# Router logits from unnormed residual tiles, and the first output projection by token halves in its second column half

## The reference

```python
x = x + merged @ w_out[l]                       # first block
xn = rms_norm(x, ffn_norm_g[l])
gate, up = jnp.split(xn @ w_gate_up[l], 2, axis=-1)
x = x + (jax.nn.silu(gate) * up) @ w_down[l]
...
x = x + g1 * gated_merge(...)                   # second block
hx2 = modulate(rmsnorm(x, norm2_g[layer]), sh2, sc2)      # h * (1 + scale) + shift
...
logits = jnp.einsum('btd,de->bte', h, w_router)           # h is hx2, 16 experts
affinity = jax.nn.softmax(logits, axis=-1)
gate, idx = lax.top_k(jnp.swapaxes(affinity, 1, 2), cap)  # 128 tokens an expert
xe = jax.vmap(lambda hb, ib: hb[ib])(h, idx)
```

## Time and profile before

| | |
|---|---|
| median of 3 runs | 2959.38 us (2957.32 to 2959.53) |
| the profiled execution | 2959.49 us |
| its span | 2957.7 us, mean granted TensorE clock 0.978 |
| busy: TensorE, VectorE, ScalarE, GpSimd | 95%, 62%, 45%, 18% |
| TensorE | 13918 matmuls, 2816.5 us |

### The profile page before, as it was taken

One profiled execution on the slowest core, in us unless ns is written; L12 is line 12 of the kernel. 1 busy time (PEld: TensorE's weight loads), 2 busy tenths in 40 slices (PEclk: granted clock), 3 DMA queues, 4 the chain that ended last, 5 costly groups with the idle time before them and its releaser, 6 DMA issues.

```text
span 2957.7 us, 34913 instructions
## 1 busy us (share of the span) xinstructions
PE 2816.5 (95%) x13918; PEld 2239.1 (76%) x13918; DVE 1823.6 (62%) x2525; ACT 1332.3 (45%) x1934; POOL 522.4 (18%) x433
## 2 busy tenths in 40 slices
PE   7999998999999999999999999999999389999997
PEld 6777776788778778888887666667888278888885
DVE  5344534788775688642323555554445669999997
ACT  4344432333233455211112666664223257777775
POOL 0001202555554011330000111111000201000000
PEclk9999999999999999999999999999999689999998
DMA  4110131345652994321211111115324579999996
GB/s 153 40 44 29 43 107 71 100 135 157 185 164 96 354 262 140 114 57 50 67 62 40 44 40 43 33 43 170 111 98 152 220 264 392 391 398 398 395 397 236
DMA packets 256485, 465.76 MB, mean 157 GB/s; under 512 B 28812, under 2 KB 135444, under 8 KB 255812
## 3 DMA queue, kind: packets, MB, share of 16 engines
q1 hardware_dynamic: 229648, 377.00, 36.3%
q0 software_dynamic: 26528, 86.50, 9.2%
q10 hardware_dynamic: 148, 0.04, 0.0%
HBM read 409.91 MB, written 53.58 MB: 157 GB/s over the span
## 4 chain that ended last, share of the span: by engine, by line
PE 88%; DVE 6%; ACT 2%; DMA 2%; issue 2%; POOL 0%; SPq 0%; POOLq 0%; DVEq 0%; ACTq 0%
PE PS L129 82%; PE PS L132 5%; DVE m L138 3%; ACT m L135 1%; DVE m L144 1%; DMA m<-in_w_down_dram 1%; ACT L135 0%; DVE m L180 0%; DVE m L183 0%; DVE m L177 0%; SPq L186 0%; POOL m L138 0%; DMA m<-h_scratch 0%; DVE m L147 0%; DMA m<-in_x_dram 0%
## 5 line engine op out<-in xcount | busy, mean ns | idle before, releaser
L129 PE MATMUL PS<-m,m 128*128 128x512 f32 (+6 forms) x12102 | 2629.8, 390 | 39.5 <-DVE m L138 24.5
L129 PEld LDWEIGHTS PS<-m,m 128*128 128x128 f32 (+3 forms) x12102 | 2035.1, 184 | 558.9 <-issue 118.7
L135 ACT ACTIVATE m<-m 128x512 fp32r<-128x512 f32 (+5 forms) x722 | 735.6, 1041 | 818.6 <-PE PS L129 432.3
L138 DVE TENSOR_TENSOR m<-m,m 128x512 fp32r<-128x512 f32 (+7 forms) x714 | 909.6, 1304 | 268.4 <-ACT m L135 230.5
L135 ACT ACTIVATE m<-PS 128x512 f32<-128x512 f32 (+4 forms) x507 | 282.2, 579 | 515.0 <-PE PS L129 343.8
L138 DVE TENSOR_TENSOR m<-PS,m 128x512 fp32r<-128x512 f32 (+1 forms) x356 | 233.1, 684 | 334.1 <-PE PS L129 300.9
L138 POOL TENSOR_TENSOR m<-m,m 128x512 f32<-128x512 f32 (+3 forms) x164 | 260.1, 1589 | 579.9 <-DVE small L147 210.2
L132 PE MATMUL PS<-ident,m 128*128 128x128 f32 x1592 | 225.2, 281 | 80.6 <-DVE m L153 36.0
L132 PEld LDWEIGHTS PS<-ident,m 128*128 128x128 f32 x1592 | 193.5, 145 | 119.3 <-DVE m L153 36.3
L135 ACT ACTIVATE m<-m,small 128x640 f32<-128x640 f32 (+4 forms) x199 | 156.3, 788 | 220.9 <-DVE small L141 153.9
L147 DVE CUSTOM_DVE_ANT_0 m<-PS,m 128x640 f32<-128x640 f32 (+4 forms) x192 | 146.4, 775 | 119.3 <-PE PS L129 119.3
(11 more groups left out here) (83 smaller groups left out, 487.8 us busy)
## 6 DMA issues: line engine op xcount, KB each, us to landing
m<-in_w_exp_gate_dram SPq DMA_DIRECT2D x64, 1024.0 KB, 8.5
m<-in_w_exp_up_dram SPq DMA_DIRECT2D x64, 1024.0 KB, 8.6
m<-in_w_exp_down_dram SPq DMA_DIRECT2D x64, 1024.0 KB, 8.1
m<-in_w_mod_dram SPq DMA_DIRECT2D x48, 512.0 KB, 3.8
m<-in_w_gate_up_dram SPq DMA_DIRECT2D x44, 512.0 KB, 6.5
m<-in_w_in_dram SPq DMA_DIRECT2D x41, 512.0 KB, 4.1
m<-in_w_in_dram SPq DMA_DIRECT2D x12, 1024.0 KB, 5.2
h_scratch<-m POOLq DMA_DIRECT2D x22, 512.0 KB, 3.6
```

What stands on the lines that cost most here:

```text
L129: return Unsent() if self.e is None else self.e.matmul(o, l, r, start=first, stop=last, **k)
L135: return Unsent() if self.e is None else self.e.activation(o, i, fn, **k)
L138: return Unsent() if self.e is None else self.e.tensor_tensor(o, a, b, op)
```

## The change

**First output projection.** The second column half is done by token halves: tiles 0 to 3 with both halves of the contraction, then tiles 4 to 7. The means, roots and scales of tiles 0 to 3, the splits of the weights for `P1`, `P2`, `P6`, `P7`, and the transposes and splits of `B11` and `B21` move into this second half. `ffn_pe` begins with `P1` and `P2`. The orders of ScalarE, VectorE and GpSimd for block 0 follow: `T1` comes before `B22`, `P5` earlier, and GpSimd makes all of `T3` before `T2`.

**Router.** TensorE transposes the residual tile itself, before its norm (`x3T`), one half as soon as that column half is added. The gain A goes into the router's weights (`wr2`), and s @ W is one product for all tiles (`shift`, from a tile `sh2b` that repeats s in all columns, made by VectorE). The transposed tile is stationary now and the 16 columns of `wr2` pass through it, so that logits come with tokens in the partitions; VectorE multiplies them by r and adds the shift (`choose`), and the copy and the transpose back are gone. For tile 7 the normed tile is made after the softmax, by ScalarE and GpSimd. A and s come as columns through two small DMAs and two small transposes.

```diff
+        WO_ORDER = [(0, 0, 6), (0, 0, 7)] + [(0, 1, i) for i in range(NT)] + [
+            (1, kg, i) for i0 in (0, 4) for kg in range(2) for i in range(i0, i0 + 4)]
...
+            for c, kg, i in WO_ORDER:
+                pe.wait_ge(*(("zu_low", i) if kg else ("at_low", i)))
+                tok_group(pe, W_O + 2 * c + kg, i, 4 * kg, 4, 8, mlhs, "wo_acc", (c, kg, i), ("x1_half", c, i))
+                if (c, kg, i) == (1, 0, 7):
+                    pe.turn, pe.kept = 0, range(4, 8)
+                    turn_first(pe, 0)
+                elif (c, kg) == (1, 1) and 4 <= i < 7:
+                    turn_first(pe, i - 3)
+            pe.turn, pe.kept = 0, ()
...
-                if c:
-                    for P in "P1 P2 P6 P7".split():
-                        gu_high(act, 0, P)
...
+                    if c and i >= 4:
+                        xn_high(act, "B11", i - 4)
+                        xn_high(act, "B21", i - 4)
+                        if i == 4:
+                            gu_high(act, 0, "P6")
+                            gu_high(act, 0, "P7")
                     act.wait_ge("x1_half", c, i)
                     square(act, x1[:, i, half512(c)], ssq[:, i, c:c + 1], "x1", i, c)
-                    if (c, i) == (1, 6):
+                    if (c, i) == (1, 3):
                         root_of(act, ssum[:, 0:4], "x1", 0)
+                        gu_high(act, 0, "P1")
+                        gu_high(act, 0, "P2")
...
-                    if (c, i) == (1, 5):
+                    if (c, i) == (1, 3):
                         x1_mean(dve, 0)
+                        inverse_of(dve, ssum[:, 0:4], rs8[:, 0:4], "x1", 0)
+                        for i_ in range(4):
+                            xt1_scale(dve, i_)
+                        gu_low(dve, 0, "P1")
+                        gu_low(dve, 0, "P2")
...
         def ffn_pe(pe):
-            for i in range(4):
-                turn_xn(pe, "B11", i)
-                turn_xn(pe, "B21", i)
-            for i in range(4):
-                turn_xn(pe, "B22", i)
             gu_product(pe, 0, "P1")
-            for i in range(4):
-                turn_xn(pe, "T1", i)
             gu_product(pe, 0, "P2")
-            for i in range(4):
-                turn_xn(pe, "T3", i)
+            for T in "T1 B22 T3".split():
+                for i in range(4):
+                    turn_xn(pe, T, i)
+            gu_product(pe, 0, "P5")
+            pe.kept = (bank_of["gu_acc", 0, "P5"],)
             for i in range(4):
                 turn_xn(pe, "T2", i)
             gu_product(pe, 0, "P7")
-            gu_product(pe, 0, "P5")
+            pe.kept += (bank_of["gu_acc", 0, "P7"],)
             for i in range(4):
                 turn_xn(pe, "T4", i)
-            for P in "P6 P4 P3".split():
+            for P in "P6 P4".split():
                 gu_product(pe, 0, P)
+            gu_product(pe, 0, "P3")
+            pe.kept = ()
...
+            gu_high(act, 0, "P5")
             root_of(act, ssum[:, 4:8], "x1", 1)
-            for i in range(4):
-                xn_high(act, "B11", i)
-                xn_high(act, "B21", i)
-            for P in "P5 P4 P3".split():
+            for P in "P4 P3".split():
                 gu_high(act, 0, P)
-            for i in range(4):
-                xn_high(act, "B22", i)
             gu_first(act, 0)
-            for i in range(4):
-                xn_high(act, "T1", i)
             gu_silu0(act, 0)
-            for T in "T3 T2 T4".split():
+            for T in "T1 B22 T3 T2 T4".split():
                 for i in range(4):
                     xn_high(act, T, i)
...
         def ffn_dve(dve):
-            inverse_of(dve, ssum[:, 0:4], rs8[:, 0:4], "x1", 0)
-            xt1_scale(dve, 0)
-            xt1_scale(dve, 1)
             x1_mean(dve, 1)
-            xt1_scale(dve, 2)
-            xt1_scale(dve, 3)
+            gu_low(dve, 0, "P5")
             inverse_of(dve, ssum[:, 4:8], rs8[:, 4:8], "x1", 1)
             for i in range(4):
-                xn_low(dve, "B11", i)
-                xn_low(dve, "B21", i)
                 xt1_scale(dve, 4 + i)
                 xn_diff_dve(dve, i)
-            for P in "P5 P4 P3".split():
+            for P in "P4 P3".split():
                 gu_low(dve, 0, P)
-            for T in "B22 T1 T3 T2 T4".split():
+            for i in range(4):
+                xn_low(dve, "T1", i)
+            for T in "B22 T3 T2 T4".split():
                 for i in range(4):
                     xn_low(dve, T, i)
-            for c in range(22):
+            gu_u2(dve, 0)
+            gu_u3(dve, 0)
+            gu_c22(dve, 0)
+            gu_c21(dve, 0)
+            for P in "P1 P6".split():
+                gu_low(dve, 1, P)
+            gu_c12(dve, 0)
+            for P in "P2 P7 P5 P4 P3".split():
+                gu_low(dve, 1, P)
+            for c in range(1, 22):
...
         def ffn_pool(pool):
-            for i in range(4):
-                xn_diff_pool(pool, "T3", i)
-                xn_diff_pool(pool, "T2", i)
-            for i in range(4):
-                xn_diff_pool(pool, "T4", i)
+            for T in "T3 T2 T4".split():
+                for i in range(4):
+                    xn_diff_pool(pool, T, i)
...
+            pool.wait_ge("o2_out", 14)
+            for a, c in enumerate((4, 3)):
+                pool.dma_start(a2raw[0:8, a, :], rows_dram[0, 1024 * c:1024 * c + 1024].rearrange("(k p) -> k p", p=128)).then_inc(
+                    *pool.landed("grows_in"))
...
+                 ("out", 7, 1, 0, 4), ("route", 6, 0, 8), ("turn", 7, 0), ("choose", 6), ("out", 7, 1, 4, 8),
+                 ("pair", 2), ("route", 7, 0, 4), ("turn", 7, 4), ("norm", 7), ("route", 7, 4, 8), ("choose", 7), ("pair", 3)]
...
+            b = pe.bank("a2_cols")
+            bank_of["a2_turned",] = b
+            pe.wait_ge("grows_in")
+            for a in range(2):
+                t = pe.transpose(PS[:, b, 8 * a:8 * a + 8], a2raw[0:8, a, :], ident[0:8, 0:8])
+            t.then_inc(*pe.did("a2_turned"))
...
+                elif what == "shift":
+                    b = pe.bank("lc_out")
+                    bank_of["lc_acc",] = b
+                    pe.wait_ge("sh2_spread")
+                    pe.wait_ge("wr_in")
+                    for k in range(8):
+                        t = pe.matmul(PS[:, b, 0:16], sh2b[:, k, :], wr[:, k, :], k == 0, k == 7)
+                    t.then_inc(*pe.did("lc_acc"))
                 elif what == "turn":
-                    pe.wait_ge("hx2", i)
-                    for k0 in (0, 4):
-                        turn4(pe, xt3[i % 3], k0, 4, "hx2_turned", (i, k0), hx2_out(i, k0))
+                    k0 = part[0]
+                    pe.wait_ge("x3_half~", i, k0 // 4)
+                    turn4(pe, x3b[i % 4], k0, 4, "x3_turned", (i, k0), x3T_out(i, k0))
...
-                elif what == "choose":
-                    b = pe.bank("lg_shifted", i)
-                    bank_of["lg_turned", i] = b
-                    pe.wait_ge("lg_out", i)
-                    pe.transpose(PS[:, b, 0:16], lgT[0:16, :], ident[0:16, 0:16]).then_inc(*pe.did("lg_turned", i))
+                    k0, k1 = part
+                    if k0 == 0:
+                        bank_of["lg_acc", i] = pe.bank("lg_raw", i)
+                    pe.wait_ge("wr_gain")
+                    pe.wait_ge(*x3T_out(i, 0))
+                    if k1 == 8:
+                        pe.wait_ge(*x3T_out(i, 4))
+                    for k in range(k0, k1):
+                        t = pe.matmul(ps("lg_acc", i)[:, 0:16], x3T[i % 2][:, k, :], wr2[:, k, :], k == 0, k == 7)
+                    if k1 == 8:
+                        t.then_inc(*pe.did("lg_acc", i))
...
+            act.wait_ge("rstd", "x3", 7)
+            act.wait_ge(f"xh_st{7 % 3}", 4)
+            act.activation(xt3[7 % 3], x3b[7 % 4], ACT.Copy, scale=r3[:, 7:8]).then_inc(*act.did("x3_scaled"))
...
+            dve.wait_ge("a2_turned")
+            dve.tensor_copy(a2cols, ps("a2_turned")[:, 0:16].rearrange("p (a k) -> p a k", k=8)).then_inc(*dve.did("a2_cols"))
+            dve.wait_ge("a2_cols")
+            dve.wait_ge("p_acc", 31)
+            dve.tensor_copy(sh2b, cols(a2cols[:, 1, :], 128)).then_inc(*dve.did("sh2_spread"))
+            dve.wait_ge("wr_in")
+            dve.tensor_tensor(wr2, wr, cols(a2cols[:, 0, :], 16), ALU.mult).then_inc(*dve.did("wr_gain"))
...
+                    if i == 7:
+                        continue
...
+                elif what == "shift":
+                    dve.wait_ge("lc_acc")
+                    dve.tensor_copy(lc, ps("lc_acc")[:, 0:16]).then_inc(*dve.did("lc_out"))
...
-                    p, l, e = ps("lg_turned", i)[:, 0:16], l3[:, i:i + 1], e3[:, i:i + 1]
-                    dve.wait_ge("lg_turned", i)
-                    dve.tensor_reduce(l, p, AX.X, ALU.max).then_inc(*dve.did("dve_order~"))
+                    p, l, e = ps("lg_acc", i)[:, 0:16], l3[:, i:i + 1], e3[:, i:i + 1]
+                    dve.wait_ge("lg_acc", i)
```

(16 more changed lines are left out.)

103 lines of the change are left out of this document (50 added, 53 removed), and 2 rows, old and new, of the table SHARED.

## The result

| | before | changed |
|---|---|---|
| median | 2959.45 us (2957.32 to 2959.92, 4 runs) | 2938.07 us (2934.08 to 2939.68, 4 runs) |
| ratio | | 0.9927 (95% interval 0.991 to 0.9944) |
| the profiled execution | 2959.49 us | 2934.08 us |
| its span, mean granted clock | 2957.7 us, 0.978 | 2932.3 us, 0.983 |

What follows compares the result with a forecast made beforehand. Taken as bound by TensorE, 88% of the chain, at the feed-forward start and the router's end: -8.0 - 7.8 + 2.0 = -13.8 from 2959.49, so 2945.7 us, range 2939 to 2953.5.

Steps and rivals of the forecast that it cites:

- rival (d): Router's end: its 7.8 us gain is lost at the experts' first products; sum -6.0, 2953.5 us; chance 6%.
- rival (e): Router products and shift: loads of 128 columns not hidden behind 16 moving ones; 0.35 us each, 2979 us; chance 8%.
- the transposes show that it does: Router products: TensorE's 128-column load hides behind the products, as for 32 transposes in 3.65 us; 0.12 us a matmul taken.
- Rival (b): Feed-forward start: bound by VectorE and GpSimd more than seen; gain there only 3 us, 2950.7 us; chance 16%.
- Term 1: Feed-forward start: work moved into the projection's second column half lets block 1 start earlier; -8.0 us.
- The walk: Feed-forward start, step by step from E, the projection's end, forecast at 498.0 us, to block 1 at E + 36.3.
- a round 2.25: Feed-forward start: each of four scale-and-difference rounds takes 2.25 us, the difference 0.95; last `T1` source at E + 13.1.
- The charge of 0.8: Feed-forward start: half of the 1.6 us that `P1` lost at half clock, charged for short bursts from E + 7.4 to E + 13.1.
- Term 2: Router's end, tile 7's last product to the top-k: 7.6 us in place of 15.44; -7.8 us.
- Term 3: Router's stage ahead of its end: cost of shift, waits and moved transposes less logits' transposes and a wait; +2.0 us.
- 1.0 of waiting: Router's stage, at the shift: TensorE waits 1.0 us while VectorE, free at 2221.2 us, takes 1.4 to spread s.
- The same exchange in `route` costs nothing: Router products of each tile: the new form with 16 moving columns costs no more than the old, at 0.12 us a matmul.

Runs made afterwards that it cites:

- experiment 9: Changed kernel, half the router products of tiles 0-6 repeated: router's stage 117.52 us; before and changed kernels without those of tiles 3-6: 101.88 and 101.71 us.
- experiment 3: Changed kernel with ScalarE's copy of the first product's result ahead of the P4 and P3 weight splits; profile only, wait ahead of `P2` 0.69 us.
- Experiment 4: Changed kernel with GpSimd's differences held back until all four of VectorE's are done; 2936.46 us, ratio 0.9923 to the kernel before.
- experiment 6: Changed kernel without the shift product; profile only, router's stage 102.95 us, its start up to tile 0's second-half gate pass 18.27 us (20.13 with shift).
- after_again: The changed kernel run and profiled once more, unedited; 2935.92 us, ratio 0.9927 to the kernel before.

## Why the prediction was wrong, point by point

**What bounds it: right.** The time changed in the two named places, and D stayed at 46 us, so rival (d) is out; rival (e) too, at its price of 0.35 or even 0.216, for a product with 128 stationary and 16 moving columns takes 0.12 us or less (0.96 for 8 in the profile after, 0.11 for each further one in experiment 9). That its load is hidden isn't shown, though. The loads of those 8 (PEld is TensorE's weight load) start as far apart as the products, 0.11 us:

```profile
2296.90 0.97 PEld L129 LDWEIGHTS PS<-m,m 128*128 128x128 f32 x8
```

It may be the loads that set this pace, with the 16 columns hidden behind them. The prediction's "the transposes show that it does" doesn't carry over, since a transpose has 128 moving columns; the price was right, the reason for it is open. The Trainium skill ("TensorE: Matmul & The Clock Gate", The mechanism) has a load overlap a running matmul only when their row groups differ, and by its figures these would take an estimated 0.13 each, load and product one behind the other. The trace has 0.11 to 0.12, with loads and products on all 128 rows and each load starting before the product ahead of it ends (ends of products are modelled), so here that sentence doesn't hold as it stands. Rival (b) was half right in its mechanism: VectorE and GpSimd do bind the stretch up to the last `T1`.

**Term 1, -8.0: measured -9.6 (-11.5 where the clock stays up at A's start).** Two errors that partly cancel, and a charge that wasn't due. *The landmark.* "Block 1 starts at 543.15 us behind a last wait" misread: that row begins with block 0's `P3`, behind a wait of 2.34 us. `P6`'s first product to the modulation product takes 68.29 us before (535.08 to 603.37) and 65.65 after (522.64 to 588.29), and as `P6`, `P4` and `P3` take 8.2, block 1 began at 535.08 + 8.2 + 2.64 = 545.9. The change removes that wait as well, and the walk should have been set against 545.9: -11.6 instead of -8.8. *The walk.* Its first steps held: moved work hidden, no wait in the second column half, first scale at E + 4.2 (4.1 forecast). The wait ahead of `P2` was half as long (0.98, not 2.0) and is hidden anyway (experiment 3). Then the step "a round 2.25" failed. It took the difference at 0.95, as if it met only the end of GpSimd's pass. But GpSimd's pass begins inside the scale and is itself held until the scale ends, so the difference always meets nearly the whole of it: 1.64, a round 2.87, and the last `T1` source at E + 14.8 instead of 13.1. Experiment 4 undoes just this and gets 1.92 a round. Behind it the walk was right again, and `P6` came at E + 29.9 where the walk has 28.1, late by as much as the last `T1` source. GpSimd, "next in line" with 0.5 us to spare, had 1.3: its last difference of `T4` ended at 519.72, and the transposes of `T4` began at 520.98. *The clock.* The charge of 0.8 was nearly all too much: the stretch from 502 to 514 us had a granted clock of 0.72, but long waits hid it, and the walk behind the last `T1` source lost 0.1. In the prediction's own sum: -8.0, -2.8 for the landmark, -0.7 for the clock, +1.8 for the rounds make -9.7.

The Trainium skill ("SBUF — State Buffer", Who interferes with whom) has a VectorE instruction with two SBUF inputs contend with a GpSimd instruction that reads SBUF, and calls the shared port pair an exclusive lock. The trace agrees with both: scales, differences and weight splits (two inputs) stretch or are stretched (0.69 to 1.64, 1.31 to 2.23), each until the other engine's pass is over, and low parts, whose one input is PSUM, take 7.25 / 12 = 0.60 beside GpSimd. I had applied it to the difference alone and not to the GpSimd pass in front.

**Term 2, -7.8: measured -8.3.** The walk of the router's end held almost step by step (reciprocal at 4.51, forecast 4.7; top-k at 7.14, forecast 7.6).

**Term 3, +2.0: measured -1.87.** This is the step that failed by most: 3.9 us, where term 1 missed by 1.6 and term 2 by 0.5, and the misses of term 3 and of term 1 are each more than the 0.9 by which the result lies outside the range. Of its 3.9 us:
- "1.0 of waiting" at the shift: 0 (experiment 6). I had 1.4 us for VectorE's spreading of s and the shift due 12.3 us into B; the copy took 0.69 and was done at 12.4, and the shift began at 12.6. With the transposes of A and s the start costs 2.3 (20.13 less 17.83) instead of 3.2.
- "0.7" ahead of tile 6's router products: 0.
- "The same exchange in `route` costs nothing": it gains. A tile's period fell from 14.17 us (between two rows of 9 transposes, 2277.68 and 2291.84) to 13.62 (`after_again`, 2262.56 to 2276.18). Of these 0.55 us, 0.2 was forecast for the logits' transpose, and rows give 0.21 (1.01 start to start with it, 0.80 without); experiment 9 gives 0.17 for the form; 0.17 aren't priced. Over seven tiles that is some 2.4 us beyond the forecast; with the 0.9 at the start and the 0.7 it makes the 3.9 within 0.1.

Between the stretches (-19.8 or -21.7) and the medians (-21.4 and -22.9) at most 3.1 us stay unassigned. The larger effect of A at a clock that stays up accounts for up to 1.9 of them; how many of the timed executions were of that kind isn't known, since only one of each kernel's runs was profiled. Untouched code has no share in it that can be seen: 2643.2 us on average with the old parts, 2643.5 with the new ones.

## What to carry to other kernels

A landmark must be an instruction that can be told apart in both kernels: cut the trace before and after at such instructions and compare stretches, for the start of a merged row may belong to the block before. When one stretch has two sizes in one program, cut it again and look at the granted clock of its untouched part: here 2.4 us of a stretch of 180 were decided before the edited code began. Where two engines lock each other out, walk both through the round, since the one that starts second is late for the first one's next step. And when small products replace others at equal price, look at the granted clock as well: here a half more of them would have taken back the gain of the whole router's part.

## What the runs showed of the hardware that was not expected

- TensorE can lose its clock while it is busy all the time. With 16, 24 and 32 matmuls of 128 stationary and 16 moving columns a tile between 48 of 512 columns and 8 transposes, the stage's granted clock was 1.00, 0.94 and 0.88; in the last case half of the added 26.9 us is clock (112 more at 0.11 are 12.4). With 32 of 16 stationary and 128 moving columns it stayed at 1.00. What makes the difference between the two forms is open.
- One stretch of untouched code has three sizes: among four waits of about 1 us the granted clock stays at 1.00 in 5 of 17 profiles and falls to 0.50 for a while in the others, which costs 2.4 or 3.1 us.
- Between executions of the same program on one core, untouched stretches differ by some 2 us: 278.15 and 276.19 us for one of them, with a granted clock of 0.95 and 0.98 from 1088 to 1160 us. Over all 17 profiles, whose code is the same there, it takes 274.6 to 280.8 us.
- A wait that is taken away can uncover another of its size: without router products VectorE was 0.7 to 1.5 us late at once, though the change itself met no wait there.
